# Hybrid trunk step on one core: an earlier request order, z kept by half chunks, and a first inverse level over all rows

## The chip, the cores and the metric

The program runs on one core of a Trainium2 chip. A core has five engines with an instruction queue each: TensorE (PE, matrix products and transposes into PSUM; its weight loads are shown as PEld), VectorE (DVE), ScalarE (ACT), GpSimd (POOL) and SyncE (SP, which here only issues DMA requests; ACT issues some too). An engine takes its instructions in the order in which they are written and waits at semaphores. The metric is device time in microseconds of one whole execution; less is better. Without the change three runs took 1837.28 us (median), from 1836.14 to 1840.30.

## The reference, cut to what matters

One layer is applied to 1024 prompt tokens and to 32 sample tokens; the kernel handles them together as 8 tiles of 128 tokens and a ninth tile of 32.

```
u    = rmsnorm(x, g_mix)
proj = u @ w_in                  # DeltaNet q,k,v | z | alpha | beta | attention q,k,v
c    = silu(causal_conv(dn_qkv)) # 4 taps per column
o_a  = rmsnorm(gated_delta_rule(l2norm(q), l2norm(k), v, g, beta), g_out_dn) * silu(z)
       # per chunk of 64 tokens and head: solve (I + A) X = rhs, A strictly lower, 64 x 64
o_b  = stick_breaking(rmsnorm(sb_q), rmsnorm(sb_k), sb_v)   # reversed product of "keep" weights
h = x + [o_a, o_b] @ w_out
h = h + relu(rmsnorm(h) @ w_up)**2 @ w_down
y = h + sigmoid(rmsnorm(h) @ w_ple_gate) * (p @ w_ple_proj)
```

Normed k, v, the last convolution rows and the final DeltaNet state are outputs too.

## The kernel before, in words

Every float32 product is made of three: each operand is split into a rounded part (hi) and its rest (lo), and hi*hi, hi*lo, lo*hi are added. POOL splits the weights (`split`, two passes over 128 x 2048 a block, lines 918 and 919; later `split_ring`).

**Projection by tokens.** x comes tile by tile (SP, line 633, three buffers). ACT squares it (1042) and takes the root (1044); DVE scales it (1500, two inputs from SBUF), PE transposes it (1943), ACT rounds it (1085), DVE makes the rest (1529). PE multiplies it with eight blocks of 256 columns of `w_in` (1922 to 1924); SP brings these (617 the first, 644 the others) into two slots. For the first four blocks each product is normed: ACT squares (1073), DVE sums and scales (1507, 1516, 1521), PE transposes (1933). The four later blocks are v (copied by ACT, 1097) and z: ACT applies silu (1106), DVE multiplies by the gain (1541), and ACT stores the tile to DRAM (1109, `z_scratch`) through two buffers.

**Convolution** (PE 1969, ACT 1138 to 1153, DVE 1567 to 1572) over twelve groups of 128 channels.

**Prompt attention.** 64 steps of scores (2001), sigmoid (1174), a scan on DVE (1596), transposes (2013) and products with value *differences* (2031). POOL makes the differences (955) from v and a copy of v shifted by one token; the shifted copy is read back from the output in DRAM by SP (714, 715 for four tiles, 718 for the rest). SP also brings the cached keys and values (699, 704) and stores the convolution tails (658).

**DeltaNet.** Nine chunks (the first is the sample) of two groups of 64 tokens, in a software pipeline: in one pass through the written loop each engine works at several chunks. A 64 x 64 inverse is made of 16 x 16 blocks: DVE inverts these in lanes (1694 to 1730), SP carries them through DRAM (780 to 808), then PE makes two levels. At the first level PE multiplies (2298), ACT copies the lower blocks through a mask `odd16` (1329, four quarters of 32 partitions), PE multiplies twice (2306, 2312), and DVE adds the lower block to the transposed inverse (1738, four quarters). SP loads z in four requests a chunk (694, 64 partitions x 256-byte pieces) before the next q and k (665).

After that come the output product, the MLP and the embedding gate, all on PE's line 2168 and its like; the change does not touch them.

The order on SP is the order in which the requests are written. It waits in front of a request for what the request needs, and every later request waits with it.

## Time and profile before

| what | value |
|---|---|
| runs, median (lowest to highest) | 1837.28 us (1836.14 to 1840.30) |
| profiled execution, its own time | 1842.09 us |
| its span, first to last instruction | 1840.4 us |
| PE busy | 1688.1 us (92%) |
| DVE, ACT, POOL busy | 718.6, 461.8, 571.3 us |
| chain that ended last: PE, DVE, DMA, issue, ACT, SP | 78, 9, 4, 3, 3, 3% of the span |

The page's chain of waits is followed back from the last instruction to whatever released each piece. 78% of it is PE: where PE never waits, only less PE work helps. The other 22% stand in the stages where PE idles: the first tiles of x, the opening of the attention, and the DeltaNet loop. Those are read one by one, with the timeline of an engine (start, duration, engine, line, tiles, shape; in square brackets the idle time just before and what ended it).

### The profile page before, as it was taken

The page shows a single profiled execution, that of the slowest core. Times are in us where ns is not written, and L with a number is a line of the kernel's source. Part 1 is how long each engine was busy: PE and PEld are TensorE (multiplying, and loading weights), DVE is VectorE, ACT ScalarE, POOL GpSimd, SP SyncE. Part 2 cuts the span into 40 slices and gives each one's busy share as a digit, 9 for nine tenths or more (in the row PEclk, how much of TensorE's full clock was granted, in tenths as well). Part 3 has the DMA queues.
Part 4 walks back from the last instruction along what each step waited for, and adds up shares of the span by engine and source line. Part 5 has one row for each costly group of instructions (what it writes and reads, how often), then busy time and mean ns, then how long its engine had stood idle before and what let it go on. Part 6 is the DMA issues. An engine that isn't in the chain of part 4 may idle for free.

```text
span 1840.4 us, 33120 instructions
## 1 busy us (share of the span) xinstructions
PE 1688.1 (92%) x14640; PEld 1595.8 (87%) x14640; DVE 718.6 (39%) x892; ACT 461.8 (25%) x906; POOL 571.3 (31%) x284
## 2 busy tenths in 40 slices
PE   5899999995899668778999999999999999999998
PEld 5799989993566456678999999999999999999898
DVE  5653033553676567762152222121212222226322
ACT  4322113222666434432132010101010101013111
POOL 2332322311100122234244343434343434342520
PEclk9999999996999779988999999999999999999999
DMA  5212311113102445432211111111111111112121
GB/s 162 64 47 70 102 62 58 70 59 127 53 2 60 130 105 109 103 82 53 85 53 46 47 46 46 46 47 46 46 46 47 46 46 47 46 46 70 46 58 49
DMA packets 203716, 118.58 MB, mean 64 GB/s; under 512 B 74481, under 2 KB 196797, under 8 KB 203580
## 3 DMA queue, kind: packets, MB, share of 16 engines
q1 hardware_dynamic: 194080, 103.54, 20.1%
q10 hardware_dynamic: 9500, 13.02, 1.9%
q8 instruction: 111, 1.82, 0.4%
q14 instruction: 25, 0.20, 0.0%
HBM read 94.69 MB, written 21.84 MB: 63 GB/s over the span
## 4 chain that ended last, share of the span: by engine, by line
PE 78%; DVE 9%; DMA 4%; issue 3%; ACT 3%; SPq 3%; POOL 0%; ACTq 0%; DVEq 0%; POOLq 0%
PE psum L2168 44%; PE psum L1969 8%; PE psum L2460 5%; PE psum L1922 3%; PE psum L1923 3%; PE psum L1924 3%; PE psum L2001 2%; PE psum L2013 2%; DVE area L1694 2%; PE psum L2031 2%; DMA area<-x_scratch 1%; DMA area<-out_dram 1%; PE psum L2479 1%; DVE area L1521 1%; DVE act_lo L1836 1%
## 5 line engine op out<-in xcount | busy, mean ns | idle before, releaser
L2168 PE MATMUL psum<-act_hi,w_round 128*128 128x352 f32 x1920 | 367.9, 324 | 0.7 <-ACT area L1351 0.4
L973 POOL TENSOR_TENSOR w_round<-w_plain,ones 128x1024 fp32r<-128x1024 f32 x80 | 175.8, 2198 | 511.7 <-DMA w_plain<-in_w_up_dram 229.3
L2168 PEld LDWEIGHTS psum<-act_hi,w_round 128*128 128x128 f32 x1920 | 319.9, 189 | 1.8 <-issue 1.0
L2168 PE MATMUL psum<-hid_hi,w_round 128*128 128x352 f32 x1344 | 257.5, 323 | 0.4 <-DVE hid_lo L1866 0.4
L2168 PEld LDWEIGHTS psum<-hid_hi,w_round 128*128 128x128 f32 x1344 | 222.3, 188 | 0.7 <-DVE hid_lo L1866 0.7
L1843 DVE TENSOR_TENSOR area<-psum,area 128x1056 f32<-128x1056 f32 x72 | 90.5, 1257 | 308.1 <-PE psum L2168 308.1
L2168 PE MATMUL psum<-act_lo,w_round 128*128 128x352 f32 x960 | 207.0, 324 | 0.0
L974 POOL TENSOR_TENSOR w_round<-w_plain,w_round 128x1024 fp32r<-128x1024 f32 x80 | 198.8, 2485 | 6.3
L1450 ACT ACTIVATE hid_hi<-area 128x1056 fp32r<-128x1056 f32 x28 | 30.4, 1087 | 589.1 <-DVE area L1859 589.1
L1922 PE MATMUL psum<-w_round,act_hi 128*128 128x256 f32 (+1 forms) x576 | 167.0, 290 | 3.9 <-ACTq L1108 3.2
L1923 PE MATMUL psum<-w_round,act_hi 128*128 128x256 f32 (+1 forms) x576 | 164.0, 285 | 0.0
L2168 PEld LDWEIGHTS psum<-act_lo,w_round 128*128 128x128 f32 x960 | 163.4, 188 | 0.0
L1924 PE MATMUL psum<-w_round,act_lo 128*128 128x256 f32 (+1 forms) x576 | 163.0, 283 | 0.0
L2168 PE MATMUL psum<-hid_lo,w_round 128*128 128x352 f32 x672 | 143.9, 323 | 0.0
L1859 DVE SCALAR_TENSOR_TENSOR area<-psum,area 128x1056 f32<-128x1056 f32 x32 | 40.2, 1258 | 240.0 <-PE psum L2168 235.0
L918 POOL TENSOR_TENSOR w_round<-w_plain,ones 128x2048 fp32r<-128x2048 f32 x14 | 50.7, 3624 | 260.8 <-PE psum L1924 156.6
L2168 PEld LDWEIGHTS psum<-hid_lo,w_round 128*128 128x128 f32 x672 | 113.8, 188 | 0.0
L1922 PEld LDWEIGHTS psum<-w_round,act_hi 128*128 128x128 f32 (+1 forms) x576 | 105.2, 183 | 5.7 <-ACTq L1108 4.0
L1969 PE MATMUL psum<-act_hi,w_round 128*128 128x352 f32 x576 | 109.1, 324 | 0.0
L1924 PEld LDWEIGHTS psum<-w_round,act_lo 128*128 128x128 f32 (+1 forms) x576 | 105.5, 183 | 0.5
L1923 PEld LDWEIGHTS psum<-w_round,act_hi 128*128 128x128 f32 (+1 forms) x576 | 105.1, 182 | 0.4
L1969 PEld LDWEIGHTS psum<-act_hi,w_round 128*128 128x128 f32 x576 | 95.9, 188 | 0.0
(293 smaller groups left out, 2433.2 us busy)
## 6 DMA issues: line engine op xcount, KB each, us to landing
w_plain<-in_w_up_dram SPq DMA_DIRECT2D x32, 512.0 KB, 4.0
w_plain<-in_w_down_dram SPq DMA_DIRECT2D x32, 512.0 KB, 3.4
w_plain<-in_w_in_dram SPq DMA_DIRECT2D x14, 1024.0 KB, 5.3
conv_scratch<-area ACTq DMA_DIRECT2D x12, 512.0 KB, 2.7
area<-in_x_prompt_dram SPq DMA_DIRECT2D x8, 512.0 KB, 3.7
w_plain<-in_cache_k_dram SPq DMA_DIRECT2D x4, 1024.0 KB, 5.5
w_plain<-in_w_out_dram SPq DMA_DIRECT2D x8, 512.0 KB, 5.0
w_plain<-in_x_prompt_dram SPq DMA_DIRECT2D x8, 512.0 KB, 5.0
```

The costliest lines, as they stand in the source:

```text
L918: own.link(pool.tensor_tensor(hi, w_raw[:, slot, :], ones[:, 0:1].to_broadcast([P, BLK]), ALU.mult))
L973: own.link(pool.tensor_tensor(hi, ring_raw(n), ones[:, 0:1].to_broadcast([P, RB]), ALU.mult))
L974: pool.tensor_tensor(lo, ring_raw(n), hi.bitcast(F32), ALU.subtract).then_inc(ring_split, 1)
L1694: own.mark(tt(terms, x.to_broadcast([LANES, b, b, b]), y.to_broadcast([LANES, b, b, b]), ALU.mult))
L1843: dve.tensor_tensor(h3, chunks_of(bank_set(tile)), h3, ALU.add).then_inc(drained, 1)
L1859: dve.scalar_tensor_tensor(out=by_chunk(wide[:, n % 2, :]), in0=chunks_of(bank_set(tile)), scalar=0.0, in1=by_chunk(wide[:, 2, :]), op0=AL ...
L1922: pe.matmul(out, hi[:, k, cols], w_h(k), start=(k == 0), stop=False)
L1923: pe.matmul(out, hi[:, k, cols], w_l(k), start=False, stop=False)
L1924: last = pe.matmul(out, lo[:, k, cols], w_h(k), start=False, stop=(k == K - 1))
L1969: last = pe.matmul(bank(base + c)[0:rows, 0:CH], w(k), a[:, k, CH * c:CH * (c + 1)], start=(k == 0 and w is lhs_hi and a is hi), stop=(k = ...
L2168: last = pe.matmul(bank(bank_set(tile) + c)[:, 0:CH], w(k), a(k)[:, CH * c:CH * (c + 1)], start=(begins and k == ks[0] and w is w_h and a ...
L2460: last = pe.matmul(bank(c)[:, 0:CH], w(k), a[:, k, CH * c:CH * (c + 1)], start=(k == 0 and w is w_h and a is act_hi), stop=(k == KT - 1 an ...
```

## The change

Five things move. (1) SP's start: the second block of `w_in` is requested after the fourth tile of x in place of after the ninth; DVE no longer waits for ten small parameter loads before its first instruction, but for the gain `g_mix` alone; PE's transpose of the parameters and ACT's copy of them come behind the first tiles. (2) SP's requests for the attention: the shifted v comes before the cached keys and the tails. (3) z lies in DRAM by half chunks, so that ACT stores each tile with two requests of 64 rows and SP loads a chunk with one. (4) ACT masks the first level in two column groups over all 128 partitions, with a two-column mask. (5) DVE adds the first level in one instruction.

```diff
-    z_dram = nc.dram_tensor("z_scratch", (T, W), F32).ap()
+    z_dram = nc.dram_tensor("z_scratch", (2 * NTT, 2, HD, W // 2), F32).ap()
-        odd16 = sb("odd16", [P, 1])
+        odd16 = sb("odd16", [P, 2])
-        def below16(x, r):
-            at = 32 * (r % 2)
-            return x[32 * r:32 * r + 32, :, at:at + 16]
+        def left16(x):
+            return x.rearrange("p m (a c) -> p m a c", a=2)[:, :, :, 0:16]
...
-            sp.dma_start(gmix_b, g_mix.broadcast_to([P, D])).then_inc(vecs_loaded, 16)
+            sp.dma_start(gmix_b, g_mix.broadcast_to([P, D])).then_inc(ab_loaded, 16)
...
+                if t == 3:
+                    sp.wait_ge(raw_free, 2)
+                    sp.dma_start(w_raw[:, 1, :].rearrange("p (k n) -> p k n", k=KT),
+                                 win[:, :, SBCOL + 256:SBCOL + 512]).then_inc(raw_loaded[1], 16)
...
-            block_in(1, 1, win[:, :, SBCOL + 256:SBCOL + 512])
...
-                n = min(real(q), HD)
-                for g in range(subs(q)):
-                    first = P * chunk(q) + HD * g
-                    z = z_dram[first:first + n, :].rearrange("i (k u e) -> u i k e", u=2, e=HD)
+                c = 2 * chunk(q)
+                if q:
+                    sp.dma_start(d_z[:].rearrange("p (g k) e -> p g (k e)", g=2),
+                                 z_dram[c:c + 2].rearrange("g u i x -> (u i) g x")).then_inc(z_loaded, 16)
...
-            sp.wait_ge(raw_free, 14 + 2)
-            for n in range(2):
-                cache_keys_in(n)
+            for u in range(2):
+                sp.wait_ge(z_stored[u], z_count(HALF))
             sp.wait_ge(v_stored, 32)
...
             sp.dma_start(v_early[1:P, 0, :], v_out[0:P - 1, :]).then_inc(vs_loaded[0], 16)
...
+            sp.wait_ge(raw_free, 14 + 2)
+            cache_keys_in(0)
             sp.wait_ge(dense_ready, NC)
             sp.dma_start(v_diff[:, 4:NT, :], v_out[4 * P - 1:TP - 1, :].rearrange("(t p) c -> p t c", p=P))\
               .then_inc(vs_loaded[1], 16)
+            sp.wait_ge(tails_c, 1)
...
+            cache_keys_in(1)
             cache_values_in(0)
...
-                act.activation(z_buf[0:rows, n % 2, :], bank(y % 2)[0:rows, 0:HC], ACT.Silu).then_inc(z_silu, 1)
+                act.activation(z_buf[0:rows, n % 2, :].rearrange("p (u k e) -> p k u e", u=2, e=HD),
+                               bank(y % 2)[0:rows, 0:HC].rearrange("p (k u e) -> p k u e", u=2, e=HD),
+                               ACT.Silu).then_inc(z_silu, 1)
...
-                act.dma_start(z_dram[P * t:P * t + rows, c:c + HC], z_buf[0:rows, n % 2, :])\
-                   .then_inc(z_stored[n % 2], 16)
+                for g in range(1 if rows < P else 2):
+                    of_chunk = slice(HD * g, min(HD * (g + 1), rows))
+                    act.dma_start(z_dram[2 * t + g, :, 0:of_chunk.stop - of_chunk.start, c // 2:(c + HC) // 2]
...
-                for r in range(4):
-                    last = act.activation(below16(d_m[:, 0:m], r), below16(mat(0, 0, m), r), ACT.Copy,
-                                          scale=odd16[32 * r:32 * r + 32, :])
+                for r in range(2):
+                    last = act.activation(d_m[:, 0:m, 32 * r:32 * r + 16], mat(0, 0, m)[:, :, 32 * r:32 * r + 16],
+                                          ACT.Copy, scale=odd16[:, r:r + 1])
...
-            dve.wait_ge(vecs_loaded, 160)
+            dve.wait_ge(ab_loaded, 16)
...
-                for r in range(4):
-                    t = below16(d_t[:, q % 2, 0:m], r)
-                    last = tt(t, below16(mat(0, 0, m), r), t, ALU.add)
-                last.then_inc(t16_made, 1)
+                t = left16(d_t[:, q % 2, 0:m])
+                tt(t, left16(mat(0, 0, m)), t, ALU.add).then_inc(t16_made, 1)
...
-            pe.wait_ge(vecs_loaded, 160)
-            pe.transpose(bank(3)[:, 0:100], param_rows[0:100, :], ident[0:100, 0:100]).then_inc(par_t, 1)
...
             turn_tile(1)
+            pe.wait_ge(vecs_loaded, 144)
+            pe.transpose(bank(3)[:, 0:100], param_rows[0:100, :], ident[0:100, 0:100]).then_inc(par_t, 1)
```

How SP's start stands in the order before (`area` holds x and the parameters, `w_plain` the raw weights; "waits" names the semaphores in front of a request):

```order
L626 DMA dn_par<-in_a_log_dram 128x8
L627 DMA dn_par<-in_dt_bias_dram 128x8
L633 DMA area<-in_x_prompt_dram 128x1024 x2
L633 DMA area<-in_x_prompt_dram 128x1024 [waits x_scaled] x3
L635 DMA ab_raw<-in_w_in_dram 128x8x16
L633 DMA area<-in_x_prompt_dram 128x1024 [waits x_scaled] x2
L633 DMA area<-in_x_sample_dram 32x1024 [waits x_scaled]
L644 DMA w_plain<-in_w_in_dram 128x8x256 [waits raw_free]
```

And with the change, where the second block (line 639) stands in front of five tiles of x instead of behind them:

```order
L629 DMA dn_par<-in_a_log_dram 128x8
L630 DMA dn_par<-in_dt_bias_dram 128x8
L636 DMA area<-in_x_prompt_dram 128x1024 x2
L636 DMA area<-in_x_prompt_dram 128x1024 [waits x_scaled]
L639 DMA w_plain<-in_w_in_dram 128x8x256 [waits raw_free]
L636 DMA area<-in_x_prompt_dram 128x1024 [waits x_scaled] x2
L642 DMA ab_raw<-in_w_in_dram 128x8x16
L636 DMA area<-in_x_prompt_dram 128x1024 [waits x_scaled] x2
L636 DMA area<-in_x_sample_dram 32x1024 [waits x_scaled]
```

SP's requests between the convolution and the attention, before (`area<-out_dram` and `act_hi_plain<-out_dram` are the shifted v, `out_dram<-area` the tails):

```order
L658 DMA out_dram<-area 36x128 [waits tails_c]
L658 DMA out_dram<-area 36x128
L699 DMA w_plain<-in_cache_k_dram 128x8x256 [waits raw_free]
L699 DMA w_plain<-in_cache_k_dram 128x8x256
L714 DMA area<-out_dram 127x512 [waits z_stored0,z_stored1,z_silu,v_stored]
L715 DMA area<-out_dram 128x3x512
L718 DMA act_hi_plain<-out_dram 128x4x512 [waits dense_ready]
```

With the change the shifted v of four tiles waits only for the stores of v and z, and the wait for the tails stands behind the rest of it:

```order
L713 DMA area<-out_dram 127x512 [waits v_stored,z_stored1,z_stored0]
L714 DMA area<-out_dram 128x3x512
L702 DMA w_plain<-in_cache_k_dram 128x8x256 [waits raw_free]
L719 DMA act_hi_plain<-out_dram 128x4x512 [waits dense_ready]
L723 DMA out_dram<-area 36x128 [waits tails_c]
L723 DMA out_dram<-area 36x128
L702 DMA w_plain<-in_cache_k_dram 128x8x256
```

ACT in one pass of the DeltaNet loop, before (1293 and 1299 are the norms of a later chunk):

```order
L1293 ACTIVATE w_plain<-psum,eps_q 128x512 [waits ss_ready]
L1293 ACTIVATE w_plain<-psum,eps 128x512
L1329 ACTIVATE area<-psum,odd 32x8x16 [waits m_ready]
L1329 ACTIVATE area<-psum,odd 32x8x16 x3
L1299 ACTIVATE w_plain<-w_plain 128x1024 [waits norms_made]
```

With the change two masks of 128 partitions stand in front of the same norm; on DVE, alike, one sum of 128x16x16 takes the place of four of 32x8x16:

```order
L1308 ACTIVATE w_plain<-psum,eps_q 128x512 [waits ss_ready]
L1308 ACTIVATE w_plain<-psum,eps 128x512
L1344 ACTIVATE area<-psum,odd 128x8x16 [waits m_ready]
L1344 ACTIVATE area<-psum,odd 128x8x16
L1314 ACTIVATE w_plain<-w_plain 128x1024 [waits norms_made]
```

Nothing else changes places in that pass.

## Rows read from the trace of the kernel before

**Rows 1.** Timeline of the start (start, duration, engine, line; idle before and releaser)
```profile
8.35 0.29 ACT L1044 ACTIVATE small<-small,eps 128x1 f32<-128x1 f32 x1
9.54 3.60 POOL L918 TENSOR_TENSOR w_round<-w_plain,ones 128x2048 fp32r<-128x2048 f32 x1 [3.33 <-DMA w_plain<-in_w_in_dram]
13.19 0.16 DVE L1497 RECIPROCAL small<-small 128x1 f32<-128x1 f32 x1 [13.19 <-DMA dn_par<-in_dt_bias_dram]
13.22 4.50 POOL L919 TENSOR_TENSOR w_round<-w_plain,w_round 128x2048 fp32r<-128x2048 f32 x1
13.39 5.42 DVE L1500 SCALAR_TENSOR_TENSOR area<-area,small 128x1024 f32<-128x1024 f32 x1
14.50 1.06 ACT L1042 ACTIVATE area<-area 128x1024 f32<-128x1024 f32 x1 [0.51 <-DMA area<-in_x_prompt_dram]
...
23.25 0.55 PE L1922 MATMUL psum<-w_round,act_hi 128*128 128x256 f32 x1 [0.71 <-issue]
```

**Rows 2.** Timeline of SP, POOL and DVE around the second weight block
```profile
40.65 14.41 SPq L644 DMA_DIRECT2D w_plain<-in_w_in_dram  x3
...
46.07 3.60 POOL L918 TENSOR_TENSOR w_round<-w_plain,ones 128x2048 fp32r<-128x2048 f32 x1 [28.35 <-DMA w_plain<-in_w_in_dram]
...
42.86 0.42 DVE L1521 TENSOR_TENSOR area<-area,heads_g 128x256 f32<-128x256 f32 x1
...
43.90 1.28 DVE L1500 SCALAR_TENSOR_TENSOR area<-area,small 128x1024 f32<-128x1024 f32 x1
...
47.80 2.16 DVE L1521 TENSOR_TENSOR area<-area,heads_g 128x256 f32<-128x256 f32 x1
...
50.06 5.41 DVE L1500 SCALAR_TENSOR_TENSOR area<-area,small 128x1024 f32<-128x1024 f32 x1
```

**Rows 3.** z stage: ACT's timeline, a piece of the chain, the page's DMA issues
```profile
233.15 0.39 ACT L1106 ACTIVATE area<-psum 128x256 f32<-128x256 f32 x1 [2.40 <-PE psum L1924]
234.11 0.33 ACTq L1109 DMA_DIRECT2D z_scratch<-area  x1
236.00 0.39 ACT L1106 ACTIVATE area<-psum 128x256 f32<-128x256 f32 x1 [2.47 <-PE psum L1924]
...
250.31 5.10 DMA z_scratch<-area
...
z_scratch<-area ACTq DMA_DIRECT2D x16, 128.0 KB, 1.7
...
at_scratch<-area SPq DMA_DIRECT2D x16, 128.0 KB, 2.7
```

**Rows 4.** Opening of the attention: the chain, PE's waits (total, times, longest), POOL's timeline
```profile
432.72 20.41 DMA area<-out_dram
...
PE psum L2031 <- POOL act_hi_plain L955: 17.1, 1, 17.1
...
453.21 5.86 POOL L955 TENSOR_TENSOR act_hi_plain<-area 128x512 f32<-128x512 f32 x4 [27.82 <-DMA area<-out_dram]
```

**Rows 5.** DeltaNet loop: two lines' durations (ns min/median/max), waits, DVE and SP timelines
```profile
L1329 ACT ACTIVATE area<-psum,odd x36: 304/358/361, 650.2 to 827.2; 32x128 f32<-32x128 f32 x32, 32x64 f32<-32x64 f32 x4
L1738 DVE TENSOR_TENSOR area<-psum,area x36: 200/283/296, 659.3 to 831.5; 32x128 f32<-32x128 f32 x32, 32x64 f32<-32x64 f32 x4
...
PE psum L2320 <- DVE area L1738: 11.5, 8, 3.7
...
DVE w_plain L1645 <- ACT w_plain L1299: 2.3, 3, 1.8
DVE area L1645 <- ACT w_plain L1299: 0.5, 2, 0.3
...
745.67 0.41 DVE L1744 TENSOR_TENSOR area<-area,psum 128x256 f32<-128x256 f32 x1
...
757.19 2.71 SPq L694 DMA_DIRECT2D area<-z_scratch  x4
762.97 0.38 SPq L665 DMA_DIRECT2D w_plain<-conv_scratch  x1
```

More of the change, by code:

```diff
@@ L601, in trunk_step, with z_count @@
         LAST_STAGED = 20
+        def z_count(n):
+            return 16 * sum(1 if tile_rows[j % NTT] < P else 2 for j in range(n % 2, n, 2)) if n < HALF else \
+                16 * (2 * NTT - 1)
         def earlier(y, lag):
@@ L654, in _ @@
                     block_in(8 + 2 * i + u, u, win[:, :, bass.ds(512 * i + 256 * u, 256)])
-            sp.wait_ge(tails_c, 1)
-            for n, dst in enumerate((conv_prompt, conv_sample)):
-                sp.dma_start(dst[0, 0].rearrange("i (m b) -> (i m) b", b=P),
-                             tails_out[36 * n:36 * n + 36, :]).then_inc(tails_stored, 16)
             def conv_qk_in(q):
@@ L705, in cache_values_in @@
                   .then_inc(vc_loaded[n % 2], 16)
-            sp.wait_ge(raw_free, 14 + 2)
-            for n in range(2):
-                cache_keys_in(n)
+            for u in range(2):
+                sp.wait_ge(z_stored[u], z_count(HALF))
             sp.wait_ge(v_stored, 32)
-            sp.wait_ge(z_silu, HALF)
-            for u in range(2):
-                sp.wait_ge(z_stored[u], 16 * NTT)
             sp.dma_start(v_early[1:P, 0, :], v_out[0:P - 1, :]).then_inc(vs_loaded[0], 16)
@@ L719, in _ @@
               .then_inc(vs_loaded[1], 16)
+            sp.wait_ge(tails_c, 1)
+            for n, dst in enumerate((conv_prompt, conv_sample)):
+                sp.dma_start(dst[0, 0].rearrange("i (m b) -> (i m) b", b=P),
+                             tails_out[36 * n:36 * n + 36, :]).then_inc(tails_stored, 16)
+            cache_keys_in(1)
             cache_values_in(0)
@@ L722, in _ @@
                 sp.wait_ge(k_stored[u], 16 * NTT)
-                sp.wait_ge(z_stored[u], 16 * NTT)
+                sp.wait_ge(z_stored[u], z_count(HALF))
             sp.wait_ge(gates_dve_done, 2)
@@ L773, in _ @@
             for u in range(2):
-                sp.wait_ge(z_stored[u], 16 * NTT)
+                sp.wait_ge(z_stored[u], z_count(HALF))
             sp.dma_start(d_sin[:, 0], state_of["in"]).then_inc(s_loaded, 16)
@@ L863, in _ @@
                 sp.wait_ge(k_stored[u], 16 * NTT)
-                sp.wait_ge(z_stored[u], 16 * NTT)
+                sp.wait_ge(z_stored[u], z_count(HALF))
                 sp.wait_ge(y_stored[u], 16 * (KT // 2 + 1 - u))
@@ L897, in _ @@
                 own.link(pool.memset(odd16[TS * g:TS * g + LB, :], 0.0))
+                own.link(pool.memset(odd16[TS * g:TS * (g + 1), 1 - g % 2:2 - g % 2], 0.0))
             keep(halves[:, 0:HD], ALU.is_gt, HD, [[0, HD]], -1)
@@ L925, in _ @@
                 split(1, u, consts_made, 3)
-            pool.wait_ge(ab_loaded, 16)
+            pool.wait_ge(ab_loaded, 32)
             own.link(pool.tensor_copy(ab_hi[:], ab_raw[:]))
@@ L942, in _ @@
             for u in range(2):
-                pool.wait_ge(z_stored[u], 16 * NTT)
+                pool.wait_ge(z_stored[u], z_count(HALF))
             own.mark(pool.memset(v_early[0:1, 0, :], 0.0))
@@ L1048, in _ @@
             square_x(0, P)
-            act.wait_ge(par_t, 1)
-            act.activation(params[:], bank(3)[:, 0:100], ACT.Copy)
             def place(y):
@@ L1086, in _ @@
                                ACT.Copy).then_inc(x_hi, 1)
+                if t == 1:
+                    act.wait_ge(par_t, 1)
+                    act.activation(params[:], bank(3)[:, 0:100], ACT.Copy)
                 if t >= 2:
@@ L1526, in _ @@
                     scale_x(t + 1, tile_rows[t + 1])
+                if t == 2:
+                    dve.wait_ge(vecs_loaded, 144)
                 dve.wait_ge(x_hi, t + 1)
@@ L1772, in gated_output @@
                 dve.wait_ge(on_read, q + 1)
-                dve.wait_ge(z_loaded, 32 * steps_to(q))
+                dve.wait_ge(z_loaded, 32 + 16 * q)
                 tt(d_on[:, 0:m], d_on[:, 0:m], d_z[:, 0:m], ALU.mult).then_inc(on_made, 1)
```

9 lines of the change are left out of this document (7 added, 2 removed).

## Prediction

> **What bounds the kernel now.** I read the page first, for the share of the chain that is PE: 78%. So I look for the stages where PE idles, and in each for the wait that ends last: the timeline of the first 60 us, the chain through the z columns, PE's waits between 420 and 470 us, and the waits of the DeltaNet loop. The reader is to see four things.
>
> At the start nothing runs on DVE before 13.19 us: its first instruction waits for the last of ten small parameter loads, though ACT had the root of tile 0 at 8.35 + 0.29 = 8.64 us. Then the first scaling meets POOL's second pass over the first weight block (13.22 to 17.72 us) and takes 5.42 us in place of 1.28; PE's first product begins at 23.25 us [rows 1, 2].
>
> At 46 us POOL splits the second weight block, which was requested only at 40.65 us, and two DVE instructions with SBUF operands stop behind it: 2.16 us for 0.42, and 5.41 for 1.28 [rows 2]. In that stretch the tiles of x go round from ACT to DVE and back without slack, so both delays are on the path.
>
> At the opening of the attention PE waits 17.1 us once, for POOL's value differences, and POOL for the shifted v, whose load took 20.41 us [rows 4]. SP asked for it behind the wait for the tails and behind two cached-key blocks.
>
> In the DeltaNet loop no engine is busy throughout. DVE waits for the norms of ACT (line 1299), which stand behind the four masks, 2.3 + 0.5 = 2.8 us in five passes, and PE waits 11.5 us in eight passes for the four DVE sums of line 1738 [rows 5].
>
> **The change, part by part.**
>
> *Start.* DVE may begin at 8.64 us plus 0.2, before POOL's first pass at 9.54 us, so the first scaling ends near 10.2 us. That gain does not reach PE whole: tile 1 of x arrives at 14.50 us [rows 1] as before, since nothing in front of it in the queue has changed; its scaling then waits for POOL's split, which still ends near 18 us. The two scalings and the second transpose are done about 1.3 us sooner, but the third tile is soon held by the split of the second block, which I expect from about 19.5 to 28 us (its request, now behind the fourth tile, leaves SP near 11 us). There PE is working through the first products, and ACT and DVE wait for it, so this split costs little. I count 0.5 us. What goes at 46 us is (2.16 - 0.42) + (5.41 - 1.28) = 5.9 us [rows 2]. Sum: 6.4 us, with 1 and 11 as ends: 1 if the collision is only displaced, 11 if the low-clock products that PE ran behind those stalls go too. The parameters' transpose and copy (0.4 and 0.25 us) move behind the second tile, where PE waits for weights or x anyway; if that cover goes, they cost their 0.65 us.
>
> *z columns.* The period of a tile is 236.00 - 233.15 = 2.85 us; silu to store takes 0.96 us, a request 0.33 us [rows 3]. Eighteen tiles now issue 34 requests in place of 18: 16 x 0.33 = 5.3 us more on ACT, hidden in its 2.4 us of idle time a tile. A buffer comes free when its store has landed. That is 1.7 us undisturbed, but 5.10 us beside a 1 MB weight load, and there it is on the chain [rows 3]. Stores in pieces of 512 bytes over 64 partitions do not occur before; the nearest row is the DeltaNet store of 128 KB over 64 partitions, 2.7 us against 1.7. I take 1.0 us of loss at the two or three disturbed stores, with 0 and 5.3 as ends (a gain is excluded: the same bytes start no earlier). The Trainium skill, "SBUF — State Buffer", section "Door 1: The DMA port swizzle", speaks against this edit: 64 partitions reach half of the DMA ports, so a tile sent as two halves moves at about half the rate. From its 196 and 328 GB/s, 128 KB would need 0.27 us more, an estimate; on two stores the z term would be 0.5 us instead of 1.0. The rows agree in direction (2.7 and 1.7 us) and show more.
>
> *Attention inputs.* The shifted v of four tiles is now asked for when the last weight block has gone out, 80 us before the first difference needs it, and the rest as soon as the convolution's last product is done (424 us), with no key block right in front. POOL starts on the four differences at about 425 us, and the first is ready before PE asks for it at 437 us: the 17.1 us go [rows 4]. What is late next is DVE. POOL's eight differences now meet the scans and the last convolution taps, which ran free at 427 to 440 us. The first four end near 431 us, under slack. The second four last 5.86 us [rows 4] by the row of the first, and can hold the fifth and sixth scans back by that much. I take 2.5 us, about half, since DVE and POOL alternate and PE asks for the sixth scan only at 441 us. Net 14.6 us; ends 11.2 and 17.1. The keys that move behind this are needed only after 583 us.
>
> *DeltaNet.* A mask costs 0.358 us for 128 elements a partition, on 32 partitions [rows 5]; I expect the same on 128, as the engine goes by elements. Four become two: 0.72 us less in front of line 1299. But DVE waits there only 2.8 us in all, 1.8 of it in one pass; so the gain is 0.72 in that pass and the whole wait, about 1.0 us together, in the other four: 1.7 us. Where DVE comes late itself, nothing is gained. The four sums take 1.18 us on end (four times about 0.29); one sum of 256 elements is like line 1744, 0.41 us [rows 5]. That saves 0.8 us a pass, but only where PE's part of the pass ends last: in three of eight passes of the chain, elsewhere SP's twelve requests do. One of the three has only 0.6 us before SP's requests end last, and I count 0.6 for each: 1.8 us. Sum 3.5 us; ends 0 (both hidden by SP's requests) and 8 x (0.72 + 0.8) = 12.2. z's one request in place of four takes 2 us off SP, which then waits until 762.97 us anyway [rows 5]: nothing; if SP had no such idle time, that would be a gain.
>
> Sum: 6.4 - 1.0 + 14.6 + 3.5 = 23.5 us. Against the profiled execution's 1842.09 us that is 1818.6; the median of the runs is 4.8 us lower, so the forecast is 1813.8 us.
>
> **Rivals.**
>
> *The collision moves.* The second split meets scalings that PE is waiting for, later than I think (if its load comes at 26 us rather than 19, it ends at 34 us, among the first norms). Against it: the DMA queues are nearly idle from 15 to 20 us. The start then gives 1 us: 23.5 - 5.4 = 18.1, 1819 us.
>
> *The wait at the attention is replaced.* The second load of shifted v is late, or DVE, stopped by POOL at each difference, holds PE longer than the second batch; the 17.1 us shrink by 9 to 10 us in place of 2.5: 16 us in all, 1821 us. For it: DVE scans already took longer beside POOL. Against it: the differences are needed one per 3 to 4 us, and each takes 1.5 us.
>
> *The DeltaNet loop gains in every pass.* If SP's long requests (1.5 to 2.2 us in some passes) shrink with z's fewer pieces, the term goes to about 10 us: 1807 us.
>
> *Slower: the half stores bind every z tile.* With two buffers a tile costs (0.96 + 0.66 + landing) / 2. It binds above 2 x 2.85 - 1.62 = 4.1 us of landing, and eats the other 24.5 us from (2.85 + 1.36) x 2 - 1.62 = 6.8 us on. At 7.5 us the stage loses 18 x 1.71 = 31 us: 1844 us. Against it: an undisturbed store of twice the size took 1.7 us, and even the worst stays under 6 us.
>
> **How the numbers follow.** Forecast 0.58, own range 1808 to 1819; collision moved 0.15; wait replaced 0.15; loop gains throughout 0.07; half stores bind 0.05. The first four lie below 1833.6 us, which is 0.2% (3.7 us, about what can be told from no change) under the median: faster 0.94, the same 0.02, slower 0.04, the last two out of the fifth case. For 8 in 10 the range goes from 1804, which takes in most of the upper ends of start and loop, to 1824, past both rivals at 1819 and 1821 with the z term at its dear end.
>
> **What would show it.** Start: DVE's first instruction before 9.5 us, the second split's POOL rows before 30 us, scalings of 1.3 us around 50 us. z: silu's idle time ended by stores no longer than before. Attention: no PE wait for POOL's differences, and POOL's first difference near 425 us on the old clock; a wait of PE for the scans of up to 6 us in its place. DeltaNet: two masks of 0.36 us and one sum near 0.4 us a pass, with the period of a pass, 22 us before, shorter by less than half a microsecond. The forecast is wrong if PE still waits over 8 us at the opening of the attention, or if the masks cost more on 128 partitions than on 32.

## The result, and the profile after

The changed kernel takes 1821.18 us (median of 4 runs, 1818.21 to 1824.06) against 1836.71 us, a ratio of 0.9911 (95% interval 0.989 to 0.9932). On another occasion, beside the experiments, it took 1824.46 us (5 runs), ratio 0.9929 (0.9915 to 0.9942). It is faster, as forecast, by 13 to 16 us; the forecast of 1813.8 us was 7.4 us too low, with the first of these times inside its range of 1804 to 1824 and the second just past it; both lie above the forecast's own range of 1808 to 1819 us. Its profiled execution took 1821.88 us, span 1820.2 us: 20 us less than that of before, which lay 5.4 us above its median, while this one lies 0.7 us above its own.

**Start.** The timeline of DVE, POOL and PE answers to [rows 1, 2] (start, duration, engine, line; L1515 is the scaling, L926 and L927 are POOL's two passes over a weight block, L1935 is PE's first product):

```profile
8.87 1.28 DVE L1515 SCALAR_TENSOR_TENSOR area<-area,small 128x1024 f32<-128x1024 f32 x1
...
15.96 3.33 DVE L1515 SCALAR_TENSOR_TENSOR area<-area,small 128x1024 f32<-128x1024 f32 x1
19.66 3.60 POOL L926 TENSOR_TENSOR w_round<-w_plain,ones 128x2048 fp32r<-128x2048 f32 x1 [1.46 <-DMA w_plain<-in_w_in_dram]
20.53 3.82 DVE L1515 SCALAR_TENSOR_TENSOR area<-area,small 128x1024 f32<-128x1024 f32 x1
21.18 0.56 PE L1935 MATMUL psum<-w_round,act_hi 128*128 128x256 f32 x1
23.34 5.46 POOL L927 TENSOR_TENSOR w_round<-w_plain,w_round 128x2048 fp32r<-128x2048 f32 x1
25.58 4.31 DVE L1515 SCALAR_TENSOR_TENSOR area<-area,small 128x1024 f32<-128x1024 f32 x1
...
48.43 1.28 DVE L1515 SCALAR_TENSOR_TENSOR area<-area,small 128x1024 f32<-128x1024 f32 x1
```

DVE begins before 9.5 us and the scaling at 48 us is undisturbed, as forecast. But the second split, now from 19.66 to 28.80 us, meets the scalings at 20.53 and 25.58, and the first split still meets the one at 15.96: 3.33, 3.82 and 4.31 us for 1.28. A good part of the collision was moved, not removed.

**z.** ACT's timeline (ACTq is the time in which its queue issues requests), pieces of the chain, and the DMA issues of 205 to 271 us (KB each, median us to landing), against [rows 3]:

```profile
218.62 1.24 ACTq L1122 DMA_DIRECT2D z_scratch<-area  x2
219.97 0.38 ACT L1115 ACTIVATE area<-psum 128x256 f32<-128x256 f32 x1 [3.56 <-DMA z_scratch<-area]
...
224.39 0.38 ACT L1115 ACTIVATE area<-psum 128x256 f32<-128x256 f32 x1 [4.04 <-DMA z_scratch<-area]
```
```profile
213.87 0.68 ACTq L1122
214.59 1.40 ACTq L1122
...
219.23 5.07 DMA z_scratch<-area
...
246.28 5.74 DMA z_scratch<-area
```
```profile
z_scratch<-area ACTq DMA_DIRECT2D x32, 64.0 KB, 2.1
```

Two requests in a row hold ACT for 1.24 to 1.26 us in 13 of 16 pairs and for 1.42 to 2.12 in the others, where one took 0.33: the second costs 0.9 us or more and not 0.33. Half the bytes land no sooner: 2.1 us for 64 KB from 64 partitions, 1.7 before for 128 KB from 128. The Trainium skill ("SBUF — State Buffer", "Door 1: The DMA port swizzle") says that 64 partitions reach half of the ports; this row agrees in direction, though it contains the wait behind the first request too.

**Attention.** PE's waits from 421 to 470 us (total, times, longest) and POOL's timeline, against [rows 4]:

```profile
PE psum L2016 <- ACT act_lo_plain L1189: 5.3, 3, 3.3
PE psum L2028 <- ACT w_plain L1204: 2.7, 1, 2.7
PE psum L2028 <- DVE act_lo_plain L1613: 1.5, 1, 1.5
```
```profile
422.18 5.17 POOL L963 TENSOR_TENSOR act_hi_plain<-area 128x512 f32<-128x512 f32 x4 [0.18 <-POOL w_plain L955]
427.31 6.82 POOL L963 TENSOR_TENSOR act_hi_plain<-act_hi_plain,area 128x512 f32<-128x512 f32 x4
```

PE's wait of 17.1 us for POOL is gone. POOL begins its differences at 422 us, and a wait of 1.5 us for the scans (L1613) is what is left in its place.

**DeltaNet.** Durations (ns, min/median/max) of the masks on ACT and the sum on DVE, and the waits from 630.3 to 805.2 us, against [rows 5]:

```profile
L1344 ACT ACTIVATE area<-psum,odd x18: 306/361/368, 631.5 to 805.6; 128x128 f32<-128x128 f32 x16, 128x64 f32<-128x64 f32 x2
L1754 DVE TENSOR_TENSOR area<-psum,area x9: 271/409/418, 639.7 to 809.4; 128x256 f32<-128x256 f32 x8, 128x128 f32<-128x128 f32 x1
```
```profile
PE psum L2313 <- DMA area<-x_scratch: 25.4, 9, 4.5
...
DVE area L1653 <- POOL area L997: 11.0, 6, 3.3
...
PE psum L2335 <- DVE area L1754: 5.1, 7, 2.9
...
DVE w_plain L1662 <- ACT w_plain L1314: 1.1, 1, 1.1
```

The operations cost what was forecast, 0.361 and 0.409 us, and PE waits for the sum 5.1 us in place of 11.5, DVE for ACT's norms 1.1 in place of 2.8. Yet the stretch from the first to the last product with x's blocks (L2313, 2298 before; x_scratch holds the inverted 16 x 16 blocks, not the tokens) lasts 174.8 us, 176.6 before.

The stages of every profiled execution, in us, worked out from the first and last rows of four lines (silu's table load, the first product for alpha and beta, the last value product, the first and the last product with x's blocks):

| kernel | start, to silu | z stage | convolution and attention | DeltaNet loop | runs, median | ratio (95%) |
|---|---|---|---|---|---|---|
| before | 217.0 | 53.7 | 312.0 | 176.6 | 1837.6 | |
| after | 211.3 | 56.0 | 296.2 | 174.8 | 1821.2 | 0.9911 (0.989-0.9932) |
| c1, after again | 212.9 | 56.5 | 298.5 | 175.5 | 1824.5 | 0.9929 (0.9915-0.9942) |
| e1 attention alone | 214.4 | 53.3 | 298.3 | 172.9 | 1821.7 | 0.9916 (0.99-0.9932) |
| e2 start alone | 210.2 | 53.4 | 313.3 | 173.0 | 1833.6 | 0.9981 (0.997-0.9993) |
| e3 z as before | 211.3 | 53.4 | 298.4 | 175.1 | 1821.2 | 0.9919 (0.9895-0.9944) |
| e4 masks, sums as before | 211.5 | 56.3 | 298.0 | 171.7 | 1819.7 | 0.9896 (0.9877-0.9914) |
| e5 SP order | 211.4 | 55.9 | 298.2 | 169.1 | 1813.5 | 0.9865 (0.985-0.9881) |
| e6 SP order, old masks | 209.9 | 56.0 | 296.9 | 165.9 | 1811.9 | 0.9866 (0.9851-0.9881) |
| e7 one z request | 211.8 | 53.3 | 296.9 | 172.0 | 1817.6 | 0.9898 (0.9882-0.9913) |
| b1 all but masks | 209.3 | 53.3 | 298.6 | 166.9 | 1811.0 | 0.9862 (0.9843-0.9882) |
| b2 one sum | 210.0 | 54.1 | 298.3 | 164.9 | 1808.8 | 0.9842 (0.9825-0.9858) |
| b3 two masks | 209.7 | 54.0 | 298.4 | 162.8 | 1809.6 | 0.9849 (0.9833-0.9865) |
| s1 second block late | 212.3 | 56.3 | 296.8 | 177.2 | 1827.1 | 0.9946 (0.9929-0.9963) |

The rows come from four occasions (before's profile and after; e1 to e4; c1 and e5 to e7; b1 to b3 and s1), and each ratio is to runs of the kernel before on the same occasion; 1837.6 us is their median beside e1 to e4.

Two things are to be seen first. The z column has two levels, 53.3 to 54.1 and 55.9 to 56.5, with nothing between. And before's row is long in places that no edit explains: e1 has its start, e1 and e2 have its loop, and they show 214.4, 172.9 and 173.0 where it shows 217.0 and 176.6. These 2.6 and 3.7 us come to 6.3, about the 5 us by which that execution lies above its median.

### The profile page after: what moved, and what is told of

Same layout as the page of the kernel before. It is cut to its first block, busy times and chain, and to the rows that moved or that the text cites. A ratio compares the mean times of both kernels' runs of the same rounds, so it can differ in the third digit from the quotient of the medians.

```text
span 1820.2 us, 33071 instructions
## 1 busy us (share of the span) xinstructions
PE 1688.2 (93%) x14640; PEld 1598.1 (88%) x14640; DVE 724.9 (40%) x865; ACT 454.4 (25%) x888; POOL 573.4 (32%) x288
## 4 chain that ended last, share of the span: by engine, by line
PE 77%; DVE 10%; DMA 3%; issue 3%; SPq 3%; ACT 3%; ACTq 0%; POOL 0%; DVEq 0%; POOLq 0%
PE psum L2183 45%; PE psum L1984 8%; PE psum L2475 5%; PE psum L1935 3%; PE psum L1936 3%; PE psum L1937 3%; PE psum L2016 2%; DVE area L1711 2%; PE psum L2028 2%; PE psum L2046 2%; DMA area<-x_scratch 1%; PE psum L2494 1%; DVE area L1536 1%; DVE area L1715 1%; DVE act_lo L1851 1%
## 5 line engine op out<-in xcount | busy, mean ns | idle before, releaser
L981 POOL TENSOR_TENSOR w_round<-w_plain,ones 128x1024 fp32r<-128x1024 f32 x80 | 169.1, 2114 | 510.9 <-DMA w_plain<-in_w_up_dram 228.3
L982 POOL TENSOR_TENSOR w_round<-w_plain,w_round 128x1024 fp32r<-128x1024 f32 x80 | 205.2, 2565 | 6.3
L1935 PE MATMUL psum<-w_round,act_hi 128*128 128x256 f32 (+1 forms) x576 | 166.6, 289 | 5.3 <-ACTq L1119 5.3
L926 POOL TENSOR_TENSOR w_round<-w_plain,ones 128x2048 fp32r<-128x2048 f32 x14 | 51.1, 3650 | 255.6 <-PE psum L1937 178.8
L1935 PEld LDWEIGHTS psum<-w_round,act_hi 128*128 128x128 f32 (+1 forms) x576 | 104.6, 182 | 6.9 <-ACTq L1119 6.3
```

Source lines behind the costliest of these rows:

```text
L926: own.link(pool.tensor_tensor(hi, w_raw[:, slot, :], ones[:, 0:1].to_broadcast([P, BLK]), ALU.mult))
L981: own.link(pool.tensor_tensor(hi, ring_raw(n), ones[:, 0:1].to_broadcast([P, RB]), ALU.mult))
L982: pool.tensor_tensor(lo, ring_raw(n), hi.bitcast(F32), ALU.subtract).then_inc(ring_split, 1)
L1935: pe.matmul(out, hi[:, k, cols], w_h(k), start=(k == 0), stop=False)
```

## The experiments

**e1: the attention's request order alone.** Before, with this edit only:

```diff
-            sp.wait_ge(tails_c, 1)
-            ...  # the two tail stores
-            sp.wait_ge(raw_free, 14 + 2)
-            for n in range(2):
-                cache_keys_in(n)
...
             sp.wait_ge(v_stored, 32)
             sp.dma_start(v_early[1:P, 0, :], v_out[0:P - 1, :]).then_inc(vs_loaded[0], 16)
...
+            sp.wait_ge(raw_free, 14 + 2)
+            cache_keys_in(0)
             sp.wait_ge(dense_ready, NC)
             sp.dma_start(v_diff[:, 4:NT, :], ...)
+            ...  # the tail stores, then the second key block
```

> The kernel before with one part of the change: SP's order of requests at the opening of the attention (the shifted v asked for as soon as v and z are stored and right after the convolution's last product, the two tail stores and the second key block behind them). z, the start and DeltaNet as before. In the two profiled executions the stretch from the last convolution product to the last attention product became 15.8 us shorter. Theory: that part alone is worth this, 1836.7 - 15.8 = 1821 us, and the trace shows no wait of PE for POOL's value differences. Rival 1: the 17.1 us wait of the profile before is longer than in an ordinary run, and the part is worth about 11 us, 1826 us, so that all parts together give the 15.5 us that the medians differ by and not the 20.2 us of the two profiles. Rival 2: the earlier load of v only works because z's new layout came with it; the wait stays above 8 us and the time above 1829 us.

Measured: 0.9916 (0.99 to 0.9932), 12.5 to 18.4 us: as much as the whole change. The attention stage is 298.3 us for 312.0 and 313.3 with the old order. The theory holds, with 13.7 to 15.0 us in that stage; rival 2 falls. Rival 1 falls with it: the wait was not an accident of one profile, since e2, with the old order, has it again (PE's waits from 424 to 475 us), and the gap between profiles and medians lies elsewhere.

```profile
PE psum L2037 <- POOL act_hi_plain L958: 17.7, 1, 17.7
```

This execution of e1 has the old start. DVE's first scaling began at 12.98 us, 0.11 us ahead of POOL's second pass, and took 1.28 us; in before it began 0.17 us behind that pass and took 5.42 [rows 1]. PE's first product came at 21.40 us here and at 23.25 there, so 1.85 of the 2.6 us by which before's start is longer stand in front of that product. This meeting, and a last parameter load that landed 0.41 us later in before, are what the rows there show as different. At 46 us e1 shows the collision of [rows 2] again (DVE, POOL and PE timelines):

```profile
12.98 1.28 DVE L1502 SCALAR_TENSOR_TENSOR area<-area,small 128x1024 f32<-128x1024 f32 x1
13.09 5.56 POOL L921 TENSOR_TENSOR w_round<-w_plain,w_round 128x2048 fp32r<-128x2048 f32 x1
...
21.40 0.56 PE L1924 MATMUL psum<-w_round,act_hi 128*128 128x256 f32 x1
...
44.42 2.26 DVE L1523 TENSOR_TENSOR area<-area,heads_g 128x256 f32<-128x256 f32 x1
...
46.79 5.39 DVE L1502 SCALAR_TENSOR_TENSOR area<-area,small 128x1024 f32<-128x1024 f32 x1
```

**e2: the start alone.** Before, with the second block's request after the fourth tile, DVE's first wait on the gain alone, and the parameters' transpose behind the second tile.

```diff
+                if t == 3:
+                    sp.wait_ge(raw_free, 2)
+                    sp.dma_start(w_raw[:, 1, :]..., win[:, :, SBCOL + 256:SBCOL + 512])
...
-            block_in(1, 1, win[:, :, SBCOL + 256:SBCOL + 512])
...
-            dve.wait_ge(vecs_loaded, 160)
+            dve.wait_ge(ab_loaded, 16)
```

> The kernel before with the start of the change alone: DVE waits for x's weights only, the parameters' transpose behind the second tile, the second weight block requested after the fourth tile of x. The first z silu came 5.7 us sooner in the trace of after. Theory: 1836.7 - 5.7 = 1831 us, the last product of the first weight block near 64 us, the scalings around 50 us at 1.28 us. Rival: the later stages swallow it (the attention's opening waits for POOL and a load, which come no sooner), and 1835 us or more.

Measured: 0.9981 (0.997 to 0.9993), 1.3 to 5.5 us, 4.0 by the medians. 1833.6 us lies between the theory's 1831 and the rival's 1835. The interval leaves out the theory's 5.7 us, which was read from the two profiles and contains before's long start; it does not leave out the 2.6 us or less of the rival, though the start stage is 4.2 us shorter than e1's and the attention stage of e2 shows at most 1.3 us of loss (313.3 for 312.0). Where PE gains is in the windows of e1 (old start) and of after (new): the columns are window, length, busy time of PE, PEld, DVE, ACT, POOL with their instructions, PE's clock, DMA share, GB/s.

```profile
24.00:40.00 16.00, 14.15 (x120) 13.45 (x118) 11.96 (x22) 8.98 (x20) 0.00 (x0) 1.00 0.44 127
40.00:56.00 16.00, 10.77 (x74) 10.09 (x75) 13.87 (x15) 6.86 (x16) 9.65 (x4) 0.89 0.55 176
```
```profile
24.00:40.00 16.00, 13.26 (x99) 12.82 (x99) 13.99 (x19) 7.31 (x15) 6.25 (x3) 0.89 0.36 103
40.00:56.00 16.00, 14.12 (x117) 13.29 (x115) 12.99 (x23) 9.24 (x21) 0.00 (x0) 1.00 0.45 141
```

From 40 to 56 us PE works 3.35 us more (43 instructions more); from 24 to 40 us, beside the moved split, 0.89 us less (21 instructions fewer). In these two executions the mean granted clock of 0.89, with a part of the 16 us at the lower level of 1.2 GHz, moves with the collision from the later window to the earlier one.

**s1: the second block late again.** After, without the `t == 3` request and with `block_in(1, 1, ...)` back behind all tiles.

> The changed kernel with the second weight block requested behind all tiles of x again, as in the kernel before; DVE's first wait and the parameters' transpose stay as changed. Splits the start's 4.0 us. Theory: the early first scaling alone is worth 0.2 to 0.5 us at the first product (21.2 us in after, 21.4 in e1 with the old start) and the request all the rest, so 3 to 4 us slower than the changed kernel's 1821 to 1824.5 us; POOL's second split meets scalings around 46 us again (5.4 us for 1.28). Rival: the early scaling is most of it, and this one costs under 1.5 us.

Measured: 0.9946 (0.9929 to 0.9963), 1827.1 us, beside 0.9929 (0.9915 to 0.9942) and 0.9911 (0.989 to 0.9932) for after on the two earlier occasions: 2.6 and 5.9 us slower by the medians, around the theory's 3 to 4 us, but the intervals overlap and the rival's 1.5 us is not excluded. The stops around 46 us are back, 2.12 us for 0.42 and 5.39 for 1.28, and still the start is 212.3 us, inside the 209.3 to 212.9 of the eleven kernels with the early request. So how the start's gain divides between the early scaling and the early request is not settled; that the request is all of it was not shown.

**e3: z as before.** After, with one store of 128 rows a tile and four loads a chunk.

```diff
-                for g in range(1 if rows < P else 2):
-                    ...  # one request for each 64 rows
+                act.dma_start(z_dram[P * t:P * t + rows, c:c + HC], z_buf[0:rows, n % 2, :])
...  # and the four loads
```

> The changed kernel with z stored and read as in the kernel before: one store request a tile instead of two, four loads a chunk instead of one. Theory: the second request of a tile (0.9 us on ACT) and the slower landings cost 2.3 us in the z stage, and SP's three further requests a chunk fall into its idle time, so 1821.2 - 2.3 = 1819 us. The prediction's size: 1.0 us, 1820 us. Rival: in the DeltaNet loop SP's requests bound the period, and the three more (about 2 us) cost 8 x 1 to 2 us there: 1827 to 1835 us, slower than after.

Measured: 0.9919 (0.9895 to 0.9944), the same as after. Its z stage is 2.6 us shorter, 53.4 us for 56.0. Its attention is 2.2 us longer than in after's profile, but like most others (298 us), and its loop is the same as after's (175.1 and 174.8). So the three more loads cost the loop nothing, and the rival falls; that the 2.6 us reach the end cannot be told from these runs.

**e7: one z request, new layout.** After, with the scratch laid out by tile, two halves of the columns and row: each tile one request again, each chunk two loads.

```diff
-    z_dram = nc.dram_tensor("z_scratch", (2 * NTT, 2, HD, W // 2), F32).ap()
+    z_dram = nc.dram_tensor("z_scratch", (NTT, 2, P, W // 2), F32).ap()
...
+                act.dma_start(z_dram[t, :, 0:rows, c // 2:(c + HC) // 2].rearrange("u i x -> i u x"),
+                              z_buf[0:rows, n % 2, :].rearrange("i (u x) -> i u x", u=2))
...  # and the two loads
```

> The changed kernel with z's scratch laid out by tile instead of half chunk: a tile is one store request on ACT again, still in pieces of 1 KB at both halves' places, and a chunk is read by two requests instead of one. Theory: the z stage lost 2.6 us to the second request of a tile (0.9 us on ACT) and not to the layout; ACT's request takes 0.33 us again and PE's convolution begins near 264.5 us on the trace's clock, as in e3, 267.3 in after. Rival: the loss came from the shorter pieces of the stores, and it stays near 267.

Measured: 0.9898 (0.9882 to 0.9913) beside c1's 0.9929 (0.9915 to 0.9942): faster by about 5.7 us, of which the z stage shows 3.2 us, 53.3 for c1's 56.5. The rest stands in the attention (1.6 us) and the loop (3.5 us), which differ by as much between other kernels with the same code there. The pieces are as short as in after (512 bytes; the 1 KB of the expectation is wrong) and the stage is as short as before, so the pieces were not the cost; the second request with its 64 partitions was. Which of the two it was, the further request or the 64 partitions, no run tells apart. ACT's timeline and the DMA issues of the same stretch in this kernel:

```profile
221.18 0.37 ACTq L1119 DMA_DIRECT2D z_scratch<-area  x1
```
```profile
z_scratch<-area ACTq DMA_DIRECT2D x16, 128.0 KB, 1.8
```

**c1: after again**, without an edit, as base for e5 to e7.

> The changed kernel once more, on the same chip as e5 to e7, as their base. If the parts add up by the traces of e1 to e4 (attention 15.9, start 4.0, z -2.6, masks and sums -1.5 to +1), it is 15 to 18 us under before: 1819 to 1822 us; the prediction's sum was 23.5.

Measured: 1824.46 us, 13.4 us under before (10.7 to 15.6): the median lies 2.5 us above the expected 1819 to 1822 us, and only the upper end of the interval reaches the 15 to 18 us that the parts gave.

**e4: masks and sums as before.** After, with four masks on 32 partitions on ACT and four sums on DVE.

```diff
-                t = left16(d_t[:, q % 2, 0:m])
-                tt(t, left16(mat(0, 0, m)), t, ALU.add).then_inc(t16_made, 1)
+                for r in range(4):
+                    t = below16(d_t[:, q % 2, 0:m], r)
+                    last = tt(t, below16(mat(0, 0, m), r), t, ALU.add)
...  # and the four masks on ACT
```

> The changed kernel with the first level's masks and sums as before: four masks on 32 partitions each on ACT and four sums on DVE, instead of two and one on 128. Theory: the loop's period is set by SP's requests and the landing of x's blocks, so the 1.5 us a pass were mostly hidden: 0.9 us in all, 1822 us, and the wait of PE for x's blocks (25.4 us in nine passes of after) falls back to about 22. Prediction's size: 3.5 us, 1824.7 us. Upper end: 8 x 1.5 = 12 us, 1833 us.

Measured: 0.9896 (0.9877 to 0.9914), no slower than after, at the most a little faster; the prediction's size is excluded. The loop takes 171.7 us for 174.8. Its waits from 632.8 to 804.6 us stand against those of after:

```profile
PE psum L2315 <- DMA area<-x_scratch: 14.3, 9, 4.4
PE psum L2337 <- DVE area L1755: 10.7, 7, 3.7
DVE area L1653 <- POOL area L997: 2.8, 2, 2.1
```

With the long sums PE waits 10.7 us for them and 14.3 for x's blocks; with the short sum 5.1 and 25.4. What was saved in front of one wait is waited at the next, and DVE itself waits 8.2 us more for POOL's decay differences (L997). The other kernels agree: with the old masks and sums PE waits 16.3 and 17.6 us for x in e1 and e2, with the new ones 23.2 to 27.7 in c1, e3, e7 and s1; only before's own long execution, 22.4, does not fit. A pass of after shows why (POOL, SP and DVE; L684 are SP's reads of the decay sums, L815 those of x's blocks):

```profile
730.97 1.13 SPq L684 DMA_DIRECT2D w_plain<-decay_scratch  x2
...
734.74 1.36 SPq L815 DMA_DIRECT2D area<-x_scratch  x2
...
735.71 1.04 POOL L997 TENSOR_TENSOR area<-w_plain,gc_all 128x512 f32<-128x512 f32 x1 [12.11 <-DMA w_plain<-decay_scratch]
...
736.78 1.08 DVE L1653 TENSOR_TENSOR area<-area,causal 128x512 f32<-128x512 f32 x1 [1.91 <-POOL area L997]
```

Both waits hang on requests that SP issues one behind the other from 727.46 us on, when DVE has finished the lanes. Earlier masks also bring POOL beside DVE: the norms' product (L1662, four and four of two forms) took 1.606 and 1.433 us on the mean in after, and 1.226 and 1.225 in e4; three of the eight took 1.99 to 2.06 us, the others 1.22 or 1.23. The lock of the shared ports that the Trainium skill tells of ("SBUF — State Buffer", "Who interferes with whom"), by which a DVE instruction with two inputs from SBUF and a POOL instruction that reads SBUF keep each other out, would do that, and these rows agree with it.

```profile
L1662 DVE TENSOR_TENSOR w_plain<-w_plain 128x1024 f32<-128x1024 f32 x4 | 6.4, 1606 | 1.2 <-ACT w_plain L1314 1.1
L1662 DVE TENSOR_TENSOR area<-w_plain 128x1024 f32<-128x1024 f32 x4 | 5.7, 1433 | 0.5 <-ACT w_plain L1314 0.3
```
```profile
L1662 DVE TENSOR_TENSOR w_plain<-w_plain 128x1024 f32<-128x1024 f32 x4 | 4.9, 1226 | 2.4 <-ACT w_plain L1314 2.4
L1662 DVE TENSOR_TENSOR area<-w_plain 128x1024 f32<-128x1024 f32 x4 | 4.9, 1225 | 1.2 <-ACT w_plain L1314 1.2
```

**e5: SP's order in a pass.** If SP's chain sets the pass, asking for x sooner must show.

```diff
                 if at(i):
                     t_in(i)
+                    x_in_blocks(i)
                 if at(i + 1):
                     lanes_in(i + 1)
-                if at(i):
-                    x_in_blocks(i)
+                if i >= 0 and at(i + 2):
+                    conv_v_in(i + 2)
...
-                if i >= -1 and at(i + 3):
-                    conv_v_in(i + 3)
```

> The changed kernel with another order of SP's twelve requests in a DeltaNet pass: the two reads of x's blocks stand right behind those of t's, the read of the lanes and conv's v behind them (before, both stood ahead of x). Theory: the pass is set by lanes made, SP's chain of requests, x's landing, PE and DVE; x is asked for 1.1 + 0.7 us sooner and the decay sums 0.7 us sooner, and each of eight passes gets 0.8 to 1.8 us shorter: 6 to 14 us, 1807 to 1815 us. Rival: DVE sets the pass by itself (norms, lane products), and PE's wait for x is slack: 1821 us, the wait only changes its name.

Measured: 0.9865 (0.985 to 0.9881) beside c1's 0.9929 (0.9915 to 0.9942): 11 us faster, the theory's size; the rival falls. The loop shows 6.4 us of it, 169.1 for c1's 175.5; of the rest 1.5 us stand in the start, which the edit does not touch. The edit also moves the reads of the lanes and of conv's v behind x, so it shows what the order is worth and not what x alone is. SP's timeline of a pass (the lanes out at 721.43 us; x's reads 5.7 us after that, 7.3 in after):

```profile
721.43 0.60 SPq L800 DMA_DIRECT2D t_scratch<-w_plain  x1
...
724.47 1.22 SPq L684 DMA_DIRECT2D w_plain<-decay_scratch  x2
725.78 1.28 SPq L808 DMA_DIRECT2D area<-t_scratch  x2
727.11 1.74 SPq L815 DMA_DIRECT2D area<-x_scratch  x2
728.95 0.58 SPq L794 DMA_DIRECT2D area<-at_scratch  x1
```

**e6: e5's order with the masks and sums of before.**

> As e5_sp_order, with the four masks on 32 partitions and four sums of the kernel before. Theory that SP's chain hid the gain of the two masks and one sum: with x sooner it shows, and this is 3 to 8 us slower than e5_sp_order. Rival: the short masks and sum gain nothing because DVE then meets POOL (the norms' product took 1.99 us beside POOL in four passes of after and 1.22 without) and waits for POOL's decay differences (11 us in after, 3 in e4): the same as e5_sp_order, or up to 3 us faster.

Measured: 0.9866 (0.9851 to 0.9881), no different from e5. So SP's chain was not the only thing that hid the short masks and sum: with x sooner they still gain nothing that can be measured, and PE's wait for x is again the longer one with them, 19.5 us in e5 for 8.9 in e6. (The long norms' products of after, in the expectation, are three and not four.)

**b1, b2, b3: everything that gained, and the two halves of the first-level edit.** b1 is after with e7's z, e5's order and the old masks and sums; b2 adds DVE's one sum, b3 ACT's two masks instead.

> What the runs so far point to: the change's start and attention order, one store request a tile for z with two reads a chunk (e7), SP's order of e5, and the first level's four masks and four sums of the kernel before. From e6 (1811.9 us) and the 2.6 to 6.9 us that one z request was worth: 1805 to 1809 us, faster than every version so far. Rival: z's three microseconds are swallowed behind it: 1811 to 1812 us.

> As b1_all_but_masks, with DVE's one sum over 128 partitions and ACT's four masks. Tells the two halves of that edit apart. Theory: the sum saves 0.77 us a pass in front of DVE's decay bound, which then waits for POOL by as much: within 2 us of b1_all_but_masks, and DVE's wait for POOL's decay differences 5 to 8 us longer in all. Rival: it gains 0.6 to 0.8 us in each of eight passes, 5 to 6 us.

> As b1_all_but_masks, with ACT's two masks over 128 partitions and DVE's four sums. Theory: ACT is 0.7 us sooner with the decays, so POOL's product with beta begins beside DVE's norms' product and slows it (1.99 us in place of 1.22): no gain or 1 to 4 us slower than b1_all_but_masks, with norms' products above 1.9 us in some passes of the trace and none in b2_one_sum. Rival: DVE waits less for ACT's norms and each pass gains up to 0.36 us: 1 to 3 us faster.

Measured: 0.9862 (0.9843 to 0.9882), 0.9842 (0.9825 to 0.9858) and 0.9849 (0.9833 to 0.9865), 1808.8 to 1811.0 us. The three cannot be told apart: neither half costs 3 us here, and a gain from either is not shown (b2's median is 2.2 us under b1's, b3's 1.4). b1 came out above its expectation of 1805 to 1809 us, at its rival's 1811: beside e6 the one z request shows 2.7 us in the z stage, but only 0.9 in the time (1811.0 for 1811.9 us, on two occasions). In b2 DVE waits 6.1 us for POOL's decay differences and in b1 6.3, so the 5 to 8 us more that I expected are not there; it is PE's wait for x that grew, from 11.5 to 18.9 us, as that for the sum fell from 10.3 to 5.1. b3 has the shortest loop, 4.1 us under b1's, but 3.9 us more behind it (1018.3 us for 1014.3 from the last product with x's blocks to the end), so that is no gain.

b3 shows no norms' product above 1.23 us, so the half that I blamed for the collision with POOL does not slow DVE by itself, and that theory falls as it stood. The two do meet in b3, in the other order. POOL's product with beta (L1003, L1005 in b3) begins 0.2 us behind DVE's norms' product there and takes 1.88 to 1.93 us in seven passes, 1.10 in most passes of e4; in the three long passes of after POOL began 0.07 to 0.14 us ahead, and DVE was held. A pass of after and one of b3 (POOL and DVE timelines):

```profile
720.35 1.04 POOL L1003 TENSOR_TENSOR area<-area,nbeta 128x512 f32<-128x512 f32 x1 [0.52 <-ACT area L1332]
720.48 1.99 DVE L1662 TENSOR_TENSOR w_plain<-w_plain 128x1024 f32<-128x1024 f32 x1
```
```profile
692.01 1.22 DVE L1660 TENSOR_TENSOR area<-w_plain 128x1024 f32<-128x1024 f32 x1
692.24 1.89 POOL L1005 TENSOR_TENSOR area<-area,nbeta 128x512 f32<-128x512 f32 x1 [0.90 <-ACT area L1330]
```

Norms' products with a mean above 1.4 us stand in all six kernels with both halves (after, c1, e3, e5, e7, s1), and in none of the eight with one or neither. As far as these kernels go it takes the two together; none has both with e5's order and e7's one request. All three beat both kernels; b2, 1808.8 us, has the lowest median.

## Why the prediction was right, and where not

*Attention, 14.6 us forecast.* Right: e1 gives 15.9 us by the medians (12.5 to 18.4), 13.7 to 15.0 in the stage. What was to be late next was DVE's scans, 2.5 us, and PE waited 1.5 us for them in after and 2.4 in e1. The rival that the wait would be replaced by another of 9 to 10 us falls.

*Start, 6.4 us forecast.* Right in mechanism and mis-sized: e2 gives 1.3 to 5.5 us. The step that failed is "this split costs little". The second split was expected at 19.5 us and came at 19.66; but DVE and PE were not idle enough there. The two scalings beside that split took (3.82 - 1.28) + (4.31 - 1.28) = 5.6 us longer than undisturbed, nearly the 5.9 us that went at 46 us, and PE worked 0.89 us less from 24 to 40 us. The rival that the collision only moves was half true. The 5.42 us of the first scaling, which the prediction shows as the old start's price, hung on 0.17 us: e1 has the old start without it.

*z, 1.0 us of loss forecast.* Mis-sized: 2.6 us in the trace (after and e3), and 3.2 between e7 and c1. The term counted a further request at the 0.33 us of a single one; the second of a pair took 0.9 us. Its cover, 2.4 us of idle time a tile, does not hold where the store's landing is on the chain, 5.07 and 5.74 us. That all of this reaches the end is not shown: e3 ends where after does.

*DeltaNet, 3.5 us forecast.* Wrong. The operations cost what was said, and DVE's wait for the norms fell by the 1.7 us that were forecast, but no pass became shorter by it: the step "0.6 for each" in three passes failed, and with it the 1.7 us as a gain in time. The four kernels with after's masks, sum and SP order beside after (c1, e3, e7, s1) have loops of 172.0 to 177.2 us; e1, e2 and e4 with the old ones have 171.7 to 173.0 (before's long execution 176.6). The saved time became DVE's wait for POOL and PE's wait for x, both at SP's queue, and in after the three long norms' products took 2.4 us more on DVE. I had seen that SP's twelve requests end last in five of eight passes, and counted a gain in the other three; e5 shows that the passes depended on the order in that queue: 6.4 us in the loop, 11 by the medians.

*The sum.* 23.5 us were forecast and 15.5 measured. By the medians of e1 and e2 the attention came out about 1.3 us above its term (15.9 for 14.6) and the start about 2.4 us short (4.0 for 6.4); z was short by 1.6 and DeltaNet by 3.5 or a little more. That is 6.2 of the 8.0 us, and each part is known to 2 or 3 us only. The subtraction of 4.8 us from the profile to the median was sound; with the four runs of the result it is 5.4, which makes the miss 7.4 us. That execution's start and loop were long, but the rows used from them were not: in e1 the stops at 46 us cost (2.26 - 0.42) + (5.39 - 1.28) = 5.95 us, 5.9 in before, and PE waited 11.4 us for the sums, 11.5 in before. So the terms failed in what follows the removed wait, and not in the reading of its size.

The forecast's own range of 1808 to 1819 us was missed. That 1821 us is the time of the rival in which the attention's wait is replaced is chance: the traces show that wait gone.

## What to carry to other kernels

A shorter operation in a software pipeline is worth nothing until it is known what the engine behind it waits for next; follow the wait to the queue that feeds it, and reorder the queue first. Put the request that the next product needs in front of those that have a pass to spare. Moving a transfer that lets one engine block another moves the collision too, so price it at the new place by the rows that stand there.

## What the runs showed that was not expected

Two requests written one behind the other cost ACT 1.24 us or more, one 0.33 to 0.40. And splitting a store in two halves of 64 partitions made the halves land in 2.1 us where the whole lands in 1.7 or 1.8. In the meetings of DVE and POOL shown here the one that began first ran on and the other was held, so 0.1 to 0.2 us decided: a scaling of DVE took 1.28 us when it began 0.11 us ahead of POOL's pass and 5.42 when it began 0.17 us behind it. Executions of the same code differ by up to 4 us in one stage: the loop, 172.9 to 176.6 us.
